# Spatial products for two token tiles at a time in a hybrid decoder trunk on one core

## The reference, cut to what matters

```python
def spatial_gating(uv, g_v, w_s, b_s):
    u, vv = uv[..., :WIDTH_B], uv[..., WIDTH_B:]
    vv = rms_norm(vv, g_v)
    vv = vv.reshape(B, S // CHUNK, CHUNK, N_GROUPS_B, GROUP_DIM_B)
    w = w_s * jnp.tril(jnp.ones((CHUNK, CHUNK), dtype=w_s.dtype))[None]
    sv = jnp.einsum('gij,bcjgd->bcigd', w, vv) + b_s.T[None, None, :, :, None]
    return u * sv.reshape(B, S, WIDTH_B)
```

## Time and profile before

| what | us |
|---|---|
| median of 3 runs | 2124.11 (2122.13 to 2124.3) |
| span of the profiled execution | 2123.8 |
| TensorE busy in it | 2088.8 (98%) |
| VectorE busy | 1459.3 (69%) |
| ScalarE busy | 924.5 (44%) |
| GpSimd busy | 1018.4 (48%) |

### The profile page before, as it was taken

The page is one execution under the profiler, slowest core; times in us unless marked ns, Lnnn a source line. Parts: engine busy times, 40 slices in busy tenths (PEclk is TensorE's granted clock), DMA queues, the critical chain, the costliest instruction groups (busy, mean ns, idle before and its releaser), DMA issues.

```text
span 2123.8 us, 30119 instructions
## 1 busy us (share of the span) xinstructions
PE 2088.8 (98%) x9850; PEld 1745.7 (82%) x9850; DVE 1459.3 (69%) x2224; ACT 924.5 (44%) x1372; POOL 1018.4 (48%) x634
## 2 busy tenths in 40 slices
PE   7999899999999999999999999999999999999999
PEld 6788788888888998888888888888878888888887
DVE  6697658888888436367777645879853421779877
ACT  6644564332332664333323346435454323463552
POOL 6865754654655004556546556759774645000000
PEclk9999999999999999999999999999999999999999
DMA  5321112333323012323333222324223323433433
GB/s 216 90 70 60 71 36 75 109 90 100 99 93 98 9 53 81 98 80 111 98 100 99 91 91 89 102 87 145 93 90 99 139 89 118 140 119 110 139 129 119
DMA packets 69313, 208.30 MB, mean 98 GB/s; under 512 B 6976, under 2 KB 7232, under 8 KB 68928
## 3 DMA queue, kind: packets, MB, share of 16 engines
q1 hardware_dynamic: 69040, 206.57, 30.1%
q10 hardware_dynamic: 144, 0.02, 0.0%
HBM read 200.28 MB, written 6.29 MB: 97 GB/s over the span
## 4 chain that ended last, share of the span: by engine, by line
PE 91%; DVE 2%; issue 2%; ACT 1%; POOL 0%; ACTq 0%; DVEq 0%; POOLq 0%
PE psum L843 23%; PE psum L845 23%; PE psum L844 23%; PE psum L1187 5%; PE psum L1186 5%; PE psum L1185 5%; PE psum L1018 3%; PE psum L867 2%; PE psum L994 1%; PE psum L995 1%; PE psum L935 1%; PE psum L925 0%; PE psum L850 0%; PE psum L856 0%; DVE small L2094 0%
## 5 line engine op out<-in xcount | busy, mean ns | idle before, releaser
L1211 POOL TENSOR_TENSOR w_buf<-raw,w_buf 128x1024 fp32r<-128x1024 f32 x270 | 659.4, 2444 | 457.5 <-ACT w_buf L1541 445.4
L843 PE MATMUL psum<-hid_buf,w_buf 128*128 128x512 f32 x1088 | 425.8, 391 | 0.0
L845 PE MATMUL psum<-hid_buf,w_buf 128*128 128x512 f32 x1088 | 423.7, 389 | 0.0
L844 PE MATMUL psum<-hid_buf,w_buf 128*128 128x512 f32 x1088 | 423.5, 389 | 0.0
L1541 ACT ACTIVATE w_buf<-raw 128x1024 fp32r<-128x1024 f32 x256 | 269.6, 1053 | 335.9 <-PE psum L845 294.0
L843 PE MATMUL psum<-h_buf,w_buf 128*128 128x512 f32 x960 | 377.0, 393 | 0.6 <-POOL h_buf L1356 0.6
L845 PE MATMUL psum<-h_buf,w_buf 128*128 128x512 f32 x960 | 374.1, 390 | 0.0
L844 PE MATMUL psum<-h_buf,w_buf 128*128 128x512 f32 x960 | 374.0, 390 | 0.0
L2283 DVE SCALAR_TENSOR_TENSOR psum<-y_buf,wdw,psum 128x512 f32<-128x512 f32 x435 | 294.9, 748 | 0.0
L844 PEld LDWEIGHTS psum<-hid_buf,w_buf 128*128 128x128 f32 x1088 | 204.4, 188 | 42.8 <-issue 0.7
L843 PEld LDWEIGHTS psum<-hid_buf,w_buf 128*128 128x128 f32 x1088 | 204.3, 188 | 42.8 <-issue 0.7
(11 more groups left out here) (311 smaller groups left out, 3068.6 us busy)
## 6 DMA issues: line engine op xcount, KB each, us to landing
raw<-weights SPq DMA_DIRECT2D x320, 512.0 KB, 3.5
w_more<-weights SPq DMA_DIRECT2D x36, 512.0 KB, 3.9
xt<-x_t SPq DMA_DIRECT2D x2, 2048.0 KB, 8.3
out_t<-xt SPq DMA_DIRECT2D x16, 256.0 KB, 2.0
...
```

Of the source, the lines that this page charges most:

```text
L843: nc.tensor.matmul(acc, lhs_hi, rhs_hi, start=first, stop=False)
L844: nc.tensor.matmul(acc, lhs_hi, rhs_lo, start=False, stop=False)
L845: return nc.tensor.matmul(acc, lhs_lo, rhs_hi, start=False, stop=last)
L1211: nc.gpsimd.tensor_tensor(dst_lo, src, dst_hi.bitcast(F32), ALU.subtract).then_inc(done, 1)
```

## The change

The products of the spatial gate are made in 8 groups that are listed in `SPATIAL`. Six of them take two tiles (0 and 1, 2 and 3, 4 and 5) and four of the eight groups of channels: 4 products of 128 columns, 64 of either tile, one product for each matrix. Tiles 6 and 7 keep 8 products of 64 columns. Each of the 8 fills bank 7 whole, as before. The scaled branch has a buffer `vz` of four tiles, and `qz` is left to the queries. ScalarE waits for spatial products only where `vz` is reused (tiles 4 to 7), and `gate_v` takes one entry of `SPATIAL`. The places change with it (`SPATIAL_AT`, `GATE_BESIDE`, `GATE_AT`). The scratch area of dynamic DMAs is set to 1024 bytes.

```diff
--- before.py
+++ after.py
@@ -110,7 +110,12 @@
 
 
 X_SQUARES = {9: (0, 1), 10: (2, 3, 4), 11: (5, 6, 7)}
-SPATIAL_AT = {(14, -1): 0, (15, -1): 1, (16, -1): 2, (19, -1): 3, (26, 0): 4, (27, 2): 5, (28, 2): 6, (29, -1): 7}
+
+SPATIAL = [((0, 1), (0, 4)), ((0, 1), (4, 8)), ((2, 3), (0, 4)), ((2, 3), (4, 8)),
+           ((4, 5), (0, 4)), ((4, 5), (4, 8)), ((6,), (0, 8)), ((7,), (0, 8))]
+SPATIAL_AT = {(15, -1): 0, (16, -1): 1, (19, -1): 2, (20, -1): 3, (27, 2): 4, (28, -1): 5, (28, 4): 6, (29, -1): 7}
+GATE_BESIDE = {14: 0, 15: 1, 26: 4, 27: 5}
+GATE_AT = {18: (2,), 19: (3,), 28: (6, 7)}
 
 Q_FIRST = (29, -1)
 SLOTS_AT = {(29, 2): 0, (29, 5): 1, (30, 0): 2, (30, 3): 3, (30, 6): 4, (31, 0): 5, (31, 3): 6, (31, 6): 7}
@@ -461,7 +466,7 @@
         c_sum, a = put("c_sum", a, [P, HALF])
         tap_early, _ = put("tap_early", a, [P, 2, HALF])
         a_tok, a = put("a_tok", a, [P, HALF])
-        rms_kept, _ = put("rms_kept", a, [P, HALF])
+        rms_kept, end_kept = put("rms_kept", a, [P, HALF])
         b_f32, _ = put("b_f32", 0, [P, 2, KT, HALF])
         pair_hid, _ = put("pair_hid", 32 * KB, [P, 2, KT, HALF])
         h_second, _ = put("h_second", 136 * KB, [P, KT, HALF])
@@ -472,7 +477,8 @@
         w_kept, _ = put("w_kept", at_sums, [P, 2, 2, 4, P])
         q_t1 = nc.alloc_sbuf_tensor_at("q_t1", [P, HEADS, P], F32R, offset=base + at_t_ring)
         q_t = [q_t0, q_t1]
-        assert max(a + 2 * KB, end_z) + base <= nc.sbuf_usable_end, (a, end_z)
+        vz, end_vz = put("vz", max(end_kept, end_z), [P, 4, HALF])
+        assert end_vz + base <= nc.sbuf_usable_end, (a, end_z)
         x_kept = nc.dram_tensor("x_kept", (P, KT, HALF), F32)
 
         diag = diag_buf[:]
@@ -925,15 +931,18 @@
                 nc.tensor.matmul(psum[:, logit_bank(n), 0:c1 - c0], qi_t[t][0:3 * ID, h, :], ki_t[0:3 * ID, c0:c1],
                                  start=True, stop=True).then_inc(logit_up, 1)
 
-            def spatial(t):
-                pe.wait_ge(z_proc, step_of(VC, t) + 1)
-                if t == 0:
+            def spatial(n):
+                tiles, (first, end) = SPATIAL[n]
+                pe.wait_ge(z_proc, step_of(VC, tiles[-1]) + 1)
+                if n == 0:
                     pe.wait_ge(ws_up, 1)
-                if t >= 1:
-                    pe.wait_ge(spat_used, t)
-                for g in range(GROUPS):
-                    mm = nc.tensor.matmul(psum[:, 7, g * GD:(g + 1) * GD], ws[:, g, :], qz[:, g * GD:(g + 1) * GD],
-                                          start=True, stop=True)
+                else:
+                    pe.wait_ge(spat_used, n)
+                size = len(tiles) * GD
+                for g in range(first, end):
+                    dst = psum[:, 7, (g - first) * size:(g - first + 1) * size].rearrange("p (t d) -> p t d", d=GD)
+                    src = vz[:, tiles[0] % 4:tiles[0] % 4 + len(tiles), g * GD:(g + 1) * GD]
+                    mm = nc.tensor.matmul(dst, ws[:, g, :], src, start=True, stop=True)
                 mm.then_inc(spat_up, 1)
 
             def sums_of_x(half):
@@ -1486,18 +1495,16 @@
                     nc.scalar.activation(q, src, ACT.Copy, scale=r).then_inc(z_read, 1)
                     act.wait_ge(z_proc, processed(s - 1) + 1 if j else s - 3)
                     act.wait_ge(z_read, s + 1)
-                    if t == 4:
-                        act.wait_ge(spat_up, 8)
                     nc.scalar.activation(qz[:], q, ACT.Square).then_inc(z_sq, 1)
                 elif c == UC:
                     nc.scalar.activation(b_tok[:, t, :], src, ACT.Gelu_apprx_tanh, scale=r).then_inc(z_read, 1)
                 else:
-                    if t:
-                        act.wait_ge(spat_up, t)
-                    act.wait_ge(z_proc, s)
-                    link(nc.scalar.activation(qz[:], src, ACT.Gelu_apprx_tanh, scale=r))
-
-                    nc.scalar.activation(src, qz[:], ACT.Square, accum_out=vsum[:, t % 2:t % 2 + 1]
+                    if t >= 4:
+                        act.wait_ge(spat_up, 2 if t < 6 else 4)
+                    act.wait_ge(z_proc, s - 1)
+                    link(nc.scalar.activation(vz[:, t % 4], src, ACT.Gelu_apprx_tanh, scale=r))
+
+                    nc.scalar.activation(src, vz[:, t % 4], ACT.Square, accum_out=vsum[:, t % 2:t % 2 + 1]
                                          ).then_inc(z_read, 1)
 
             def keys_out(t):
@@ -2058,14 +2065,18 @@
                 for job in beside:
                     job()
                 dve.wait_ge(r_up, n + 1)
-                V.scalar_tensor_tensor(out=qz[:], in0=qz[:], scalar=r_v[:, t % 2:t % 2 + 1], in1=gvb[:],
+                V.scalar_tensor_tensor(out=vz[:, t % 4], in0=vz[:, t % 4], scalar=r_v[:, t % 2:t % 2 + 1], in1=gvb[:],
                                        op0=ALU.mult, op1=ALU.mult).then_inc(z_proc, 1)
 
-            def gate_v(t):
-                dve.wait_ge(spat_up, t + 1)
-                groups = psum[:, 7, :].rearrange("p (g d) -> p g d", g=GROUPS)
-                link(V.tensor_tensor(groups, groups, bs[:][:, :, None].broadcast_to([P, GROUPS, GD]), ALU.add))
-                V.tensor_tensor(b_tok[:, t, :], b_tok[:, t, :], psum[:, 7, :], ALU.mult).then_inc(spat_used, 1)
+            def gate_v(n):
+                tiles, (first, end) = SPATIAL[n]
+                dve.wait_ge(spat_up, n + 1)
+                groups = psum[:, 7, :].rearrange("p (g n) -> p g n", g=end - first)
+                bias = bs[:, first:end][:, :, None].broadcast_to([P, end - first, len(tiles) * GD])
+                link(V.tensor_tensor(groups, groups, bias, ALU.add))
+                u = b_tok[:, tiles[0]:tiles[-1] + 1, first * GD:end * GD].rearrange("p t (g d) -> p g t d", d=GD)
+                gates = psum[:, 7, :].rearrange("p (g t d) -> p g t d", t=len(tiles), d=GD)
+                V.tensor_tensor(u, u, gates, ALU.mult).then_inc(spat_used, 1)
 
             def index_scores(n):
 
@@ -2216,13 +2227,13 @@
                     for job in beside:
                         job()
                 else:
-                    if t % 4:
-                        beside = (*beside, lambda: gate_v(t - 1))
+                    if s in GATE_BESIDE:
+                        beside = (*beside, lambda: gate_v(GATE_BESIDE[s]))
                     process_v(s, t, nth_rms, beside)
                 for k in X_SQUARES.get(s, ()):
                     add_x_squares(1, k)
-                if s in (18, 28):
-                    gate_v(3 if s == 18 else 7)
+                for n in GATE_AT.get(s, ()):
+                    gate_v(n)
 
                 for _ in range(TOPK_PLAN.get(s, 0)):
                     topk((2, 3), 4 * rounds)
@@ -2638,7 +2649,8 @@
         "w_dw": np.asarray(inputs["od_w_dw"])[0].reshape(CONV, KT, P).transpose(2, 1, 0),
     }
     arrays = {name: np.ascontiguousarray(a) for name, a in arrays.items()}
-    nc = bacc.Bacc("TRN2", target_bir_lowering=False, num_devices=1)
+    nc = bacc.Bacc("TRN2", target_bir_lowering=False, num_devices=1,
+                   dynamic_dma_scratch_size=1024)
     args = [nc.dram_tensor(name, a.shape, mybir.dt.from_np(a.dtype), kind="ExternalInput").ap()
             for name, a in arrays.items()]
     out_t = nc.dram_tensor("out_t", (KT, P, SEQ), F32, kind="ExternalOutput").ap()
```

## The result

The changed kernel takes 2130.78 us in the median of 5 runs (2128.73 to 2131.73), the kernel before, measured beside it, 2123.99 (2122.03 to 2124.3): 1.0036 times as long, 95% interval 1.0026 to 1.0047. By the medians that is 6.8 us slower and 0.28 us beyond the upper end of my range; the time forecast was 2127.1.

What follows compares the result with a forecast made beforehand. TensorE was taken as the bound, busy 2088.8 of 2123.8 us. 2124.11 + 0.4 (new waits against savings) + 2.6 (one clock fall) = 2127.1 us; forecast's own range 2124.8 to 2129, overall range 2121.5 to 2130.5.

Steps and rivals of the forecast that it cites:

- The rival that passes grow with columns: Spatial products: 128-column passes take longer, so no 5.1 us gain and shorter waits; about 2126 to 2129 us, chance 0.04.
- the 5.1 us: Spatial products on TensorE, taken alone: 14.4 us before, 9.3 after, with six groups at 0.95 and two at 1.80.
- the stands: TensorE idle for the gate of the group before: 3.5 us ahead of step 20, 4.4 us behind step 28.
- The 0.39 of the first group: TensorE's wait for VectorE at the first spatial group, ahead of step 14; expected to go, 0.39 us.
- so it moves by the 3.0 us of that point: Third group's gate, behind step 18's keys: follows the weight-piece chain from step 15's end, ending 3.1 us earlier at 138.35.
- Second half: Tiles 4 to 7: 1.7 us lead, 4.4 us wait for tile 6's gate, 0.74 and 1.4 regained; -0.6 us.
- The waits alone: Whole kernel without clock effects: 0.2 us gained in the first half, -0.6 in the second; 0.4 us slower.
- I take one fall, behind the longer stand, at 2.6 us.: TensorE's clock drops once, after the 4.4 us wait behind step 28, costing 2.6 us.
- the first rival: Clock falls behind both long waits, in step 20 and steps 29 to 30: 2.9 and 2.6 us, 2130.0 us, chance 0.24.
- The 1.28 us of wait for the rotated queries: End of step 20: TensorE's old wait for GpSimd takes up the 1.2 us lag, leaving the first half at 0.0.
- The stretch from 242 us: Ten us at granted clock 1.00 with TensorE busy 8.31; taken as evidence that not every gap lowers the clock.

Runs made afterwards that it cites:

- e5: Changed kernel with unread products filling both long TensorE waits, 18 ahead of step 20 and 17 ahead of tile 7; 2126.60 us, 1.0014 of the kernel before.
- e3: Changed kernel with third spatial group ahead of step 18, its gate behind step 16's keys, tile 6's gate ahead of step 28's indexer sums; 2119.84 us, 0.9984 of before.
- e7: e3 with each product of 128 columns made as two of 64, 16 passes per group; 2119.70 us, 0.9984 of the kernel before.
- e9: The kernel of e3 once more, timed beside e10 and e11; 2119.72 us, 0.9987 of the kernel before.
- e10: The kernel of e7 (unpaired products) once more, timed beside e9 and e11; 2119.31 us, 0.9985 of the kernel before.
- e2: Changed kernel with only VectorE's gate of tile 6 moved ahead of step 28's indexer sums; 2124.04 us, 1.0004 of the kernel before.
- e1: Changed kernel with only the third spatial group moved ahead of step 18 and its gate behind step 16's keys; 2125.96 us, 1.0015 of the kernel before.
- e6: Changed kernel with 17 unread products filling only the second long wait, ahead of tile 7; 2127.12 us, 1.0017 of the kernel before.
- e11: The changed kernel itself once more, timed beside e9 and e10; 2130.84 us, 1.0039 of the kernel before.
- e8: e3 with tiles 6 and 7 paired too, as two groups of 4 products of 128 columns; 2119.47 us, 0.9986 of the kernel before.
- e12: e3 with nine unread products ahead of the ninth attention slot's value products, in a 2.21 us TensorE wait; 2119.83 us, 0.9987 of the kernel before.

## Why the prediction was wrong, by its own steps

- **The products.** The pace was right: eight passes of 128 columns go at the pace of 64 (0.81 us between 139.00 and 139.81 in e5, 0.85 predicted). The rival that passes grow with columns is out. But the 5.1 us do not come through even without the stands: paired against unpaired is 1.1 and 1.4 us at the scores and nothing in the medians (e3 and e7, e9 and e10). The 0.39 of the first group did not go: the new first group waits 0.40 for its scaling. The gate's second instruction kept its 0.69 us, as costed; it is six of the eight gates that read `b_tok` in runs of 64, not half of them.
- **First half. A wait mis-sized: "so it moves by the 3.0 us of that point".** The stand came, at its place and with its releaser. It was 4.63 us, not 3.5. By the bare times the gate seems to have ended where it was predicted (138.26 for 138.35) and TensorE to have had more lead than predicted (133.77 for 134.85 at the end of step 19), but 1.38 us of both is the late marker of before. Counted from it, TensorE's lead was 2.65 us (predicted 2.95), VectorE's low parts came 1.6 earlier (112.42 for 115.43; predicted 1.9), and the gate came only 1.9 earlier (136.85 for 140.12), where the prediction had 3.1. The gate moved about as far as VectorE's own queue had moved at the low parts, and not with the chain of weight pieces from the end of step 15. Without the low clock TensorE would have been 1.0 us late at the transposition behind step 20 (predicted 0.0; the group's start from the marker, 51.77, and e5's 6.74 for the rest, against 57.49 before).
- **Second half.** Predicted 4.4, measured 4.19; the chain of ScalarE and VectorE is the one listed (rows above: 0.69, 0.63, 0.36; 0.48, 0.68, 0.69, 0.69). e2 shows that it was the cause: with the gate ahead of that chain the wait is 0.94. The lag added here without the low clock is some 0.7 us, for 0.6 predicted.
- **The waits alone.** Predicted 0.4 us slower, measured 1.7 at the scores (7.06 less the 5.32 of the falls), of which the gate of the first half is nearly all of the error. In the medians e5, with 0.9 us of overrun in it, is 3.0 us slower than before (0.05% to 0.24%), which leaves out 0.4 too.
- **The clock. This step failed: "I take one fall, behind the longer stand, at 2.6 us."** Both stands were followed by a fall, which was the first rival with 0.24. The first fall cost 1.6 us: 0.9 in the group (1.70 for 0.81) and the rest in step 20 (6.68 us from 140.10 to 146.78, for 6.04 before). The 1.28 us of wait for the rotated queries, which was to absorb the lag, was used up by a lag of 2.4 us that was there without the low clock, and no cushion was left. The second cost 3.7: 1.6 in the group (3.26 for 1.70), 0.7 in the transpositions (1.56 for 0.85) and the rest in step 29. Their sum is 5.3 us, where I had 2.6; the rival's 5.5 was right in sum, though it gave the first 2.9 and the second 2.6. The second was the dearer, behind the shorter stand. The stretch from 242 us, on which I rested the chance that a stand is forgiven, begins right behind a wait of 2.21 us (ended at 241.75) and has one of 1.24 in it; it says nothing of one of 4. And the lower level is in that trace a third time, near 1555 us, behind two waits of 0.58 and 0.38 us; the prediction missed it when it said twice.
- **The Trainium skill** ("TensorE: Matmul & The Clock Gate", section "Why this matters for your kernels") has it that idle gaps between bursts bring the lower clock back. For these two stands the traces agree (0.72 and 0.55 behind them, 1.00 with the same stands filled), and its rule gave the better number. The prediction should have leant on it more: the only row against it was of another kind of gap.
- **The base.** I took the span of 2123.8 to stand beside the median 2124.11 "with 0.3 beside it". In every run with a span on record the time is 1.7 or 1.8 us over it (2131.67 and 2129.9, 2120.09 and 2118.4), so the profiled execution of before lasted about 2125.5 us by that rule, more than the median. This did not move the forecast, which adds a difference to the median. It did hide the late marker, and with it 1.4 us of every lead that I compared afterwards.
- **The range.** Its upper end lay 0.5 us above the first rival's 2130.0, while single runs of the changed kernel spread from 2128.73 to 2131.73. That the time fell 0.28 us outside and not just inside is chance; that the forecast's clock and its first wait were too cheap is not.

## What to carry to other kernels

Work taken from the bounding engine becomes a lead, and a lead runs into the next wait that had slack: here a gate at the end of another engine's queue, harmless until then. Such a releaser moves with its own engine's queue: take its lead from there. Before removing such work, list the waits behind it with their slack, and move their releasers forward in the same edit (e3: one place in `SPATIAL_AT`, two entries of `GATE_AT` and one call, 11 us). A stand of 4 us in dense products costs its length and then a few microseconds at half the clock; price both. Before times of two traces are compared, take a marker ahead of the change from each.

## What the runs showed of the chip

- Stands of 3.4 to 4.6 us of TensorE in dense work were followed by a low granted clock each time, in after, e1, e2, e6 and e11. Of shorter ones, 0.94 us (e2, e3) was not and 1.93 us (e8) was. A wait of 1.1 us ahead of `project(16)` was followed by one in e3, e5, e6 and e9 and was not in after, e1, e2, e8, e11 and e12; one of 2.21 us near 240 us was in eight profiles and was not in five. So below 3.4 us the same wait goes both ways.
- The cost of the low clock behind one and the same stand differs between executions: 1.6 to 2.6 us behind the stand of 4.63, 1.5 to 3.7 behind that of 4.19.
- A stand that is filled with products whose sums nobody reads keeps the clock (e5, e6): 4.7 us in the medians for the two places together.
- With the clock at 1.00 a pass costs 0.11 us with 64 columns (1.70 us for 16) and 0.10 with 128 (0.81 for 8), and one of the fillers' passes of 512 columns 0.23 (4.19 us between 134.81 and 139.00 for 18).
- Executions of one kernel differ by up to 4.4 us here (e5, 2123.70 to 2128.08). One short fall of the clock near 1555 us, present in nine of the fourteen profiles, is worth some 1.6 of that, and what is lost ahead of step 14 another 1.2 (the marker is at 87.58 in e7 and at 86.38 in e10, the same kernel).
